# Expert weights requested in the order of use: gate and up of an expert, then down of the preceding one

## What is computed

```python
for gi in range(N_GROUPS):            # 4 groups of 8 experts; each token goes to 2 of the 32
    h = silu(einsum('nd,edf->nef', xt, e_wg[gi])) * einsum('nd,edf->nef', xt, e_wu[gi])
    out = out + einsum('nef,efd->nd', h * comb[:, gi, :, None], e_wd[gi])
```

## Time and profile before

| | us |
|---|---|
| median of three runs | 1383.91 |
| the profiled execution | 1382.05 |
| its span, first to last instruction | 1380.3 |
| start of the experts' products | 861 |
| end of the last down product | 1347.5 |
| mean granted clock of TensorE, share of full | 0.953 |
| PE busy | 1213.5 (88%) |
| DVE busy | 415.2 (30%) |
| ACT busy | 328.5 (24%) |
| mean GB/s over the span | 206 |

### The profile page before, as it was taken

The page is one execution under the profiler, slowest core; times in us unless marked ns, Lnnn a source line. Parts: engine busy times, 40 slices in busy tenths (PEclk is TensorE's granted clock), DMA queues, the critical chain, the costliest instruction groups (busy, mean ns, idle before and its releaser), DMA issues.

```text
span 1380.3 us, 23959 instructions
## 1 busy us (share of the span) xinstructions
PE 1213.5 (88%) x10652; PEld 897.0 (65%) x10652; DVE 415.2 (30%) x712; ACT 328.5 (24%) x549; POOL 98.5 (7%) x141
## 2 busy tenths in 40 slices
PE   4999998999989989999999998997878787888880
PEld 3899998986778768999999877332223332333330
DVE  4336631334162254233342414110001101000115
ACT  5444322333232244222232313110000100000102
POOL 3000000000000000000000001132111111111100
PEclk9999999998998899999999999999999999999995
DMA  7110104000212463232232837899999999999976
GB/s 224 62 31 1 33 6 155 4 3 27 72 64 92 117 180 114 70 91 83 78 92 85 301 151 276 348 399 393 418 394 419 420 419 420 420 419 418 420 300 210
DMA packets 114786, 283.97 MB, mean 206 GB/s; under 512 B 25011, under 2 KB 72325, under 8 KB 90106
## 3 DMA queue, kind: packets, MB, share of 16 engines
q1 hardware_dynamic: 108586, 270.60, 52.7%
q0 software_dynamic: 5440, 9.46, 1.8%
q10 hardware_dynamic: 656, 2.36, 0.4%
HBM read 274.11 MB, written 15.61 MB: 210 GB/s over the span
## 4 chain that ended last, share of the span: by engine, by line
PE 62%; DMA 22%; DVE 6%; SPq 5%; ACT 2%; issue 2%; POOL 1%; POOLq 0%; DVEq 0%; ACTq 0%
DMA slot<-in_e_wu_dram 20%; PE bank L1308 7%; PE bank L1257 6%; PE bank L1258 6%; PE bank L1259 6%; PE bank L627 5%; SPq L575 5%; PE bank L634 3%; PE bank L1419 2%; PE bank L1420 2%; PE bank L1421 2%; PE bank L1483 2%; PE bank L1487 2%; PE bank L1485 1%; DMA slot<-expert_outputs 1%
## 5 line engine op out<-in xcount | busy, mean ns | idle before, releaser
L627 PE MATMUL bank<-slot,xs 128*64 128x512 f32 x512 | 252.3, 642 | 74.8 <-DMA slot<-in_e_wu_dram 73.7
L628 PE MATMUL bank<-slot,xs 128*64 128x512 f32 x512 | 253.6, 644 | 0.0
L627 PEld LDWEIGHTS bank<-slot,xs 128*64 128x64 f32 x512 | 70.3, 146 | 216.3 <-issue 215.0
L1257 PE MATMUL bank<-xnh,wh 128*128 128x256 f32 (+1 forms) x448 | 133.6, 298 | 0.5 <-ACT bt_ogm L2186 0.5
L1258 PE MATMUL bank<-xnl,wh 128*128 128x256 f32 (+1 forms) x448 | 133.3, 298 | 0.0
L1259 PE MATMUL bank<-xnh,low 128*128 128x256 f32 (+1 forms) x448 | 133.3, 297 | 0.0
L927 DVE TENSOR_TENSOR h<-sg,bank 64x512 f32<-64x512 f32 x32 | 21.7, 680 | 338.5 <-ACT sg L824 338.5
L824 ACT ACTIVATE sg<-bank 64x512 f32<-64x512 f32 x32 | 19.0, 593 | 439.5 <-PE bank L628 439.5
L2278 DVE TENSOR_TENSOR low<-ring,wh 128x1536 fp32r<-128x1536 f32 (+1 forms) x45 | 90.0, 2005 | 99.0 <-ACT wh L1939 89.5
L634 PE MATMUL bank<-slot,ht 128*64 128x512 f32 x512 | 116.9, 598 | 1.0 <-DVE ht L946 1.0
L1939 ACT ACTIVATE wh<-ring 128x1536 fp32r<-128x1536 f32 (+1 forms) x45 | 75.4, 1679 | 47.2 <-PE bank L1303 20.8
(11 more groups left out here) (483 smaller groups left out, 2279.3 us busy)
## 6 DMA issues: line engine op xcount, KB each, us to landing
slot<-in_e_wg_dram SPq DMA_DIRECT2D x64, 1024.0 KB, 28.4
slot<-in_e_wu_dram SPq DMA_DIRECT2D x64, 1024.0 KB, 27.8
slot<-in_e_wd_dram SPq DMA_DIRECT2D x64, 1024.0 KB, 26.9
ring<-in_w_in_dram SPq DMA_DIRECT2D x13, 1024.0 KB, 8.8
ring<-in_w_in_dram SPq DMA_DIRECT2D x24, 512.0 KB, 4.3
ring<-in_w_branch_dram SPq DMA_DIRECT2D x24, 256.0 KB, 4.8
kvs<-in_cache_mem_k_dram SPq DMA_DIRECT2D x8, 512.0 KB, 5.2
kvs<-in_cache_mem_v_dram SPq DMA_DIRECT2D x8, 512.0 KB, 4.4
```

What stands on the lines that cost most here:

```text
L627: pe.matmul(out[64:128, :], tok, wg[:, FF * k:FF * k + FF], start=(k == 0), stop=(k == KD - 1))
L628: mm = pe.matmul(out[0:64, :], tok, wu[:, FF * k:FF * k + FF], start=(k == 0), stop=(k == KD - 1))
L1257: pe.matmul(part, w_h, xh_(k, cols), start=(k == 0), stop=False)
```

## The change

Three things change together. SP asks for gate and up of expert e and then for down of e - 1 (behind the wait for ("d", e - 4)), instead of down of e; a last round asks for down of 31. The list of PE's steps and PE's loop lose their special order at the last expert: `down(30)` now comes after `gate_up(31)`, as for all others. DVE's loop and its list lose it too. Sizes, slots, numbers of instructions and bytes are the same.

```diff
         pe_m = Steps(sem("pe_m"), [x for e in range(EX + 1) for x in
-                                   ([("t", 0)] if e == 0 else []) + ([("d", e - 1)] if e == EX - 1 else [])
-                                   + ([("gh", e), ("gu", e)] if e < EX else []) + ([("t", e + 1)] if e + 1 < EX else [])
-                                   + ([("d", e - 1)] if e and e != EX - 1 else []) + ([("ht", e)] if e < EX else [])])
+                                   ([("t", 0)] if e == 0 else []) + ([("gh", e), ("gu", e)] if e < EX else []) + ([("t", e + 1)] if e + 1 < EX else [])
+                                   + ([("d", e - 1)] if e else []) + ([("ht", e)] if e < EX else [])])
...
-            for e in range(3, EX):
-                for f in range(2):
-                    pe_m.wait(sp, ("gu" if f else "gh", e - 3))
-                    load(e, 0, (f,))
-                    load(e, 1, (f,))
-                pe_m.wait(sp, ("d", e - 3))
-                load(e, 2)
+            for e in range(3, EX + 1):
+                if e < EX:
+                    for f in range(2):
+                        pe_m.wait(sp, ("gu" if f else "gh", e - 3))
+                        load(e, 0, (f,))
+                        load(e, 1, (f,))
+                if e > 3:
+                    pe_m.wait(sp, ("d", e - 4))
+                    load(e - 1, 2)
                 if e == 10:
...
             for e in range(EX + 1):
-                if e == EX - 1:
-                    down(e - 1)
                 if e < EX:
                     gate_up(e)
                 if e + 1 < EX:
                     act_e.wait(pe, ("xs", e))
                     turn_in(e + 1)
-                if e and e != EX - 1:
+                if e:
                     down(e - 1)
                 if e < EX:
                     turn_h(e)
```

## The result

| | before | after |
|---|---|---|
| median, us | 1382.82 (5 runs) | 1369.55 (5 runs, 1367.98 to 1374.05) |
| ratio, 95% interval | | 0.9913 (0.9891 to 0.9936) |
| span of the profiled execution | 1380.3 | 1372.3 |
| first gate product to last down product starts | 861.0 to 1346.8 | 862.2 to 1339.6 |
| mean granted clock | 0.953 | 0.953 |

The change is faster by 0.87%: 12.0 us of 1383 by the ratio, 8.8 to 15.1 by its interval. In the two profiled executions the spans differ by 8.0 us.

A forecast was written before the change was run, and what follows sets the result against it. DMA of expert weights was taken to bound the stage, leaving gains only where DMA idles or after the last bytes. 5.6 + 0 + 3.6 = 9.2 us off 1383.9 gave 1374.7, range 1371 to 1380.5.

The forecast's parts named there:

- The hole: DMA idle at 877 to 882 us, SP waiting for down of expert 0; closing it gains 5.6 us (4.7 to 6.3).
- My reading by bytes: Size of the gap at 877 to 882 us from missing bytes: 4.7 us, and a restart of roughly 1 us more.
- The tail: After the last weights land: gate-up (31) ready two MB earlier, less work left behind the last byte; gains 3.6 us.
- later rounds: Rounds with DMA saturated: gate and up requested before the previous down; cost nothing, 0 us.
- the down weights just in time: In each round, down weights landing behind gate and up are in time by 0.8 us at the least; cost nothing.
- The token lists' place in the stream: Load of line 603 goes out one 2 MB chunk earlier; between -1.9 and +1.9 us, taken as 0.
- The sum: Whole kernel: 5.6 + 0 + 3.6 = 9.2 us less, from 1383.9 to 1374.7; chance 0.64.
- (c): Rival: 1.9 us of the token lists or part of 3.9 us at 926 go too; 1371.7; chance 0.07.
- (a): Rival: the hole closes, the tail gains nothing as down (30) lands late; 1378.3; chance 0.13.
- (b): Rival: the hole closes but comes again at a later limit, only the tail counts; 1380.3; chance 0.08.
- (d): Rival: PE becomes the bound through its clock, 24 us more; 1398.7; chance 0.04.
- (e): Rival: SP is held by a full queue, not by waits, so no gain; 1383.9; chance 0.04.

The follow-up runs named there:

- b: Kernel before with only the requests of experts 4 to 9 in the new order, old end kept: 1376.71 us, ratio 0.9969 to the kernel before.
- j: The kernel before, unedited, run once more for a second profile: 1379.97 us.
- d: Kernel before with only the end changed: gate and up of 31 requested before down of 30, usual product order at the last expert: 1381.13 us, ratio 0.9995.
- e: Kernel before with the new request order only from expert 21 on and the usual product order at the last expert: 1377.59 us, ratio 0.9967.
- i: Kernel before with gate and up of 30 and 31 each requested before the preceding down, usual product order at the last expert: 1377.46 us, ratio 0.9963.
- c: Kernel before with the new request order from expert 4 to 30, old end kept: 1373.93 us, ratio 0.9952 to the kernel before.
- a: The changed kernel again, unedited, against the kernel before: 1370.57 us, ratio 0.9923.
- f: The changed kernel again, unedited, in a later group, against the kernel before: 1371.63 us, ratio 0.9934.
- g: Changed kernel without the load of the token lists, tile filled with a constant: 1369.75 us, ratio 0.9909 to the kernel before.
- h: Changed kernel with scatter and load of the token lists only in the branch for experts over 64 tokens: 1364.01 us, ratio 0.9869 to the kernel before.

## Why the prediction was right or wrong, point by point

**The hole: mechanism right, and no run shows the size to be wrong.** Requests, times and the filled window came as foretold. b measured 4.3 us (2.4 to 6.2) where I had taken 5.6. My reading by bytes, 4.7 and roughly 1 for the restart, is borne out by the trace of before, where 106 and then 262 GB/s in the two us behind the window make 1.1 us of missing bytes, 5.8 in all:

```profile
882.00:883.00 1.00, 1.00 (x7) 0.43 (x8) 0.50 (x2) 0.00 (x0) 0.03 (x1) 1.00 0.85 106
883.00:884.00 1.00, 1.00 (x8) 0.31 (x6) 0.00 (x0) 0.00 (x0) 1.00 (x1) 1.00 0.68 262
```

The ten profiles with the token lists say the same, when the stage is cut at the landing of the last bytes, which leaves out what PE has still to do after it:

| | us from the first gate product to the last landing | us from there to the end of the last product |
|---|---|---|
| before, j (hole, old end) | 481.0, 482.9 | 5.6, 7.4 (with the slow products of j) |
| d (hole, end changed for 31 alone) | 482.5 | 3.9 |
| e, i (hole, new end) | 480.2, 482.0 | 2.1, 2.0 |
| b, c (no hole, old end) | 476.5, 476.7 | 5.7, 5.1 |
| after, a, f (no hole, new end) | 475.9, 476.4, 474.5 | 2.1, 2.1, 2.1 |

With the hole the first column is 481.7 in the mean, without it 476.0, and the groups don't overlap: 5.7 us, by their scatter good to some 1.4, an estimate.

**The tail: size right, cause told by half.** I gave 3.6; e and i measured 4.6 and 5.1 (both intervals reach down to 2.5 or below), and the second column has 5.6 to 2.1, 3.5 us. The course I wrote for the end of the whole change came nearly to the letter (12.3 us from gate and up of 31 to the end, measured 12.0). But it has PE free at 1331.5, and I gave no reason for that and put the gain down to the move of 31 and to the product order. d shows that these do not suffice: they win nothing that can be measured, as PE was still working off expert 30. PE was free in time since the change moves 30 ahead of down of 29 as well, which I had listed under "later rounds" at no cost and no gain. That the sum came out in spite of it was luck. The earlier trace rows begins at 1330.65 with PE busy; had I followed it back to the last wait, it would have led to the landing for 30, at 1321.5.

**The later rounds and the down weights just in time: right by the traces.** 420 GB/s against 419, one wait of 0.5 us, and b and c 0.2 us apart in the first column. The runs of c leave some 1.4 us open (2.0 less than b in their mean, 0.6 of it at the end). The token lists' place in the stream: 2.4 us of bytes missing at 990 to 1010 against 1.9 to 2.2 before; right at 0.

**The sum and the range: the step that failed is the base of the sum, and a range that had no room for its scatter.** The sum of gains, 9.2 us, is in the intervals of all three measurements of the change (ratios of 0.9913, 0.9923 and 0.9934, 9.1 to 12.0 us with half-widths near 3), and the table has 5.7 + 3.5 = 9.2. All 18 runs of the changed kernel against the 48 of the kernel before that ran beside them give 10.2 us (8.8 to 11.6). What I took it from was the median of three runs, 1383.9, while the kernel before has its median at 1381.4 over all: the base was 2.5 us high, and 1381.4 - 9.2 = 1372.2. Of the 5.1 us between forecast and result, 2.5 are this base, 1.4 are that the five runs of the result have their median at 1369.55 and all 18 at 1370.9, and 1.2 are what the gain is over 9.2 by the medians, which is within its interval.

Single runs scatter with a standard deviation of 3.1 us before and 2.5 us after. From these, a median of three and one of five together scatter by some 2.5 us, an estimate. I had noted the spread of 5.6 us, and yet reckoned the low end, 1371.0, from the mechanism (c) alone, 3.7 us below the forecast, with nothing for either median. Part of the miss is thus bad luck in two draws. Whether the gain is nearer 9 or nearer 11 is open; the parts add up to 4.3 + 4.6 = 8.9, or 9.4 with i.

**The rivals.** (a), tail without gain, is what d alone does, but the whole change doesn't. The Trainium skill, in "DMA: Bandwidth & Descriptors", section "Queues, rings and completion order", has completion not first in, first out per issuing engine. Here that cost nothing: in the tail the loads landed in order, after the change at 1330.6, 1333.1 and 1338.1 for three of the last four (the trace has no landing of the third). (b), the hole comes again, fell with b. (c), more than forecast: the dips did not go with the change, they had to be taken away (g, h), and then gave about what was put down for them, 1.9 and, with the other, 5.5 to 7.6 us. (d), PE bound through its clock: not here, 0.953 in both, and products of up to 1083 ns instead of 592 as before. The Trainium skill's section "HAM oscillation — how this bites in real kernels" ("TensorE: Matmul & The Clock Gate") has work restart at half speed behind a wait for data. The trace of before agrees in the main: behind a wait of 1.8 us at 1173.9 the first two products still take 610 and 590 ns, the next ones up to 1060. In the saturated stretch that shows no price, as DMA stays the bound. (e) fell with the first window.

## What to carry to other kernels

With DMA saturated, the order of requests was worth something in two places here: where the stream still has holes, because a wait in the issuing queue holds back a load whose slot is already free, and at the end, where what lands last decides what work is left. To price the end, follow PE's work back to its last real wait; the piece that ended that wait must come sooner, not only the one that is used last. Before a forecast is set against a median of three runs, put the scatter of that median into the range. And small transfers in a saturated stream cost here the bytes that they displaced: work for a case that hardly occurs belongs in the branch for it.

## What the runs showed of the hardware that I had not expected

The start of the experts' stage, ahead of which no line of the work was changed, lay between 855.8 and 865.3 us in the profiles. I have no cause for it. Of an early start a part is kept: with 855.8 against 861.0 the last bytes landed at 1338.7 against 1341.9.

The load of the token lists, 144 KB, holds SP's queue for 24 to 26 us (977.95 to 1003.79 before, 970.46 to 994.7 after), some ten times the 2.14 us of a 1 MB load in a full queue, and yet the stream loses only about 2 us by it.

In the last 8 us ahead of the last landing the DMA engines no longer work as one. After the change they move 279 GB/s in 1330 to 1331 and then 164, 139, 123, 74, 82, 41 and 16 in the us that follow, some 0.9 MB that would take 2.2 us at 420 GB/s, an estimate; before the change it is the same, from 287 in 1334 to 1335 down to 74 in 1340 to 1341. Why some engines lag is not shown, and nothing was tried to even them out.
